# A later second gather and an earlier split of the first gathered rows in a mixture-of-experts block

## What is computed

```python
def hierarchical_moe(h2, w_rg, w_re, w_gate, w_up, w_down):
    ...
    eid = g_sel[:, None] * EXPERTS_PER_GROUP + top_i
    ...
    def expert_block(args):
        xb, e = args
        return (jax.nn.silu(xb @ w_gate[e]) * (xb @ w_up[e])) @ w_down[e]
```

## Time and profile before

| | us |
|---|---|
| median of 3 runs | 1263.93 |
| lowest and highest run | 1262.71, 1267.04 |
| span of the profiled execution | 1263.3 |
| TensorE busy in the span | 1220.1 |
| VectorE busy | 959.5 |
| ScalarE busy | 681.5 |
| GpSimd busy | 257.5 |

### The profile page before, as it was taken

The page is one execution under the profiler, slowest core; times in us unless marked ns, Lnnn a source line. Parts: engine busy times, 40 slices in busy tenths (PEclk is TensorE's granted clock), DMA queues, the critical chain, the costliest instruction groups (busy, mean ns, idle before and its releaser), DMA issues. The chain is left out here.

```text
span 1263.3 us, 18788 instructions
## 1 busy us (share of the span) xinstructions
PE 1220.1 (97%) x7332; PEld 1013.2 (80%) x7332; DVE 959.5 (76%) x1173; ACT 681.5 (54%) x819; POOL 257.5 (20%) x193
## 2 busy tenths in 40 slices
PE   4799999999999999999989999999999999999997
PEld 1799888888788887888778888888888888788883
DVE  1756554432578888666789999999999999999977
ACT  3932212111456666422256777777777777677734
POOL 0000000001100000100020634535355272622110
PEclk9899999999999999999989999999999999999999
DMA  9649844435566775431379999999999999999949
GB/s 380 252 178 311 286 138 142 170 121 169 185 221 185 156 189 133 151 110 51 137 264 358 379 386 392 375 389 380 382 385 377 385 375 395 382 363 378 384 150 359
DMA packets 96620, 344.36 MB, mean 273 GB/s; under 512 B 18522, under 2 KB 46866, under 8 KB 68883
## 3 DMA queue, kind: packets, MB, share of 16 engines
q1 hardware_dynamic: 75603, 311.91, 67.8%
q10 hardware_dynamic: 11696, 14.44, 3.9%
q0 software_dynamic: 9232, 16.80, 3.6%
HBM read 314.24 MB, written 39.34 MB: 280 GB/s over the span
## 5 line engine op out<-in xcount | busy, mean ns | idle before, releaser
L2262 DVE TENSOR_TENSOR w_low<-raw,w_high 128x2048 fp32r<-128x2048 f32 x128 | 291.7, 2299 | 6.0 <-ACT w_high L2194 5.1
L2194 ACT ACTIVATE w_high<-raw 128x2048 fp32r<-128x2048 f32 x128 | 240.8, 1908 | 4.9 <-PEq L1388 3.8
L2076 PE MATMUL p_gu<-w_high,x_high 128*128 128x512 f32 x504 | 202.5, 402 | 0.0
L2078 PE MATMUL p_gu<-w_high,x_low 128*128 128x512 f32 x504 | 197.2, 391 | 0.0
L2077 PE MATMUL p_gu<-w_low,x_high 128*128 128x512 f32 x504 | 196.3, 390 | 0.0
L2262 DVE TENSOR_TENSOR w_low<-arena,w_high 128x2048 fp32r<-128x2048 f32 x62 | 142.6, 2303 | 25.5 <-ACT w_high L2194 25.5
L2134 POOL DMA_INDIRECT y_rows<-arena,row x31 | 66.9, 2158 | 311.1 <-DVE arena L2293 309.6
L2194 ACT ACTIVATE w_high<-arena 128x2048 fp32r<-128x2048 f32 x62 | 118.2, 1906 | 0.0
L2078 PEld LDWEIGHTS p_gu<-w_high,x_low 128*128 128x128 f32 x504 | 94.6, 188 | 20.9
L2077 PEld LDWEIGHTS p_gu<-w_low,x_high 128*128 128x128 f32 x504 | 94.9, 188 | 18.0
L2076 PEld LDWEIGHTS p_gu<-w_high,x_high 128*128 128x128 f32 x504 | 95.2, 189 | 17.7
(11 more groups left out here) (426 smaller groups left out, 2532.1 us busy)
## 6 DMA issues: line engine op xcount, KB each, us to landing
raw<-in_w_gate SPq DMA_DIRECT2D x64, 1024.0 KB, 7.9
raw<-in_w_up SPq DMA_DIRECT2D x64, 1024.0 KB, 8.1
arena<-in_w_down SPq DMA_DIRECT2D x62, 1024.0 KB
raw<-in_w_ada SPq DMA_DIRECT2D x24, 1024.0 KB, 7.6
x<-qk_rows SPq DMA_DIRECT2D x6, 1664.0 KB, 8.3
raw<-in_w_chunks SPq DMA_DIRECT2D x9, 1024.0 KB, 5.7
qk_rows<-x SPq DMA_DIRECT2D x18, 512.0 KB, 2.6
mod<-x ACTq DMA_DIRECT2D x48, 128.0 KB, 3.2
```

The lines of the kernel that those rows point to most:

```text
L2076: pe.matmul(dst, high, w_high, start=start, stop=False)
L2078: return pe.matmul(dst, low, w_high, start=False, stop=stop)
L2194: act.activation(x.high[i % SPLITS][:], x.raw[b][:, :], ACT.Copy).then_inc(high_ok, 1)
L2262: dve.tensor_tensor(x.low[i % SPLITS][:], x.raw[home(n, j)][:, :], x.high[i % SPLITS][:], ALU.subtract).then_inc(low_ok, 1)
```

## The change

Three lines are moved and one wait is new. The gather of expert 1 is no longer issued at the end of `mix_and_route` but at the start of GpSimd's stream in `main_experts`, behind a wait for the landing of the gather of expert 0. On ScalarE the two halves of expert 0's rows are split before chunk 3 instead of after it.

```diff
@@ mix_and_route, gpsimd
                 pool.wait_ge(listed_ok, 1)
-                for n in range(2):
-                    gather(pool, a, s, n)
+                gather(pool, a, s, 0)
                 pool.wait_ge(coded, 4)
@@ main_experts, gpsimd
             steps = Counter(pool, over_ready)
+            pool.wait_ge(gathered[0], 16)
+            gather(pool, a, s, 1)
             pool.wait_ge(x_turned, 1)
             gather(pool, a, s, 2)
@@ main_experts, scalar
             split(0, 2)
+            x_split_halves(0)
             split(0, 3)
-            x_split_halves(0)
             split(1, 0)
```

## The result

| | before | changed |
|---|---|---|
| median, us (20 runs each) | 1263.93 | 1267.49 |
| lowest run | 1261.57 | 1262.94 |
| span of the profiled execution | 1263.3 | 1262.2 |

What follows compares the result with a forecast made beforehand. TensorE, nearly without idle time through the expert loop, was taken to bound the kernel. Gains and costs of 0 plus a 1.2 us stall from the moved gather gave 1263.93 + 1.2 = 1265.1 us, range 1262.6 to 1267.3.

Steps and rivals of the forecast that it cites:

- First gather, gain 0: Seam between routing and experts: expert 0's gather lands no sooner, has 2.7 us to spare behind TensorE's filler; gain 0.
- Block boundary: Boundary at 648.04 does not move, since TensorE's event, not GpSimd's second issue, is last; gain 0, at most 0.3 us.
- ScalarE's exchange, cost 0: Halves ahead of chunk 3 still start at 652.02; chunk 3 comes later but has 4.5 us of cover; cost 0.
- The moved gather: Expert 1's gather: issue 649.4 to 651.2, landing 8.0 us later at 659.2, wanted at 658.03; stall 1.2 us.
- The rival by which the gather would interleave at once: Moved gather shares the queue with weights at once or finds it lighter, lands near 654.1, hidden; 1263.9 us, chance 0.26.
- They move with TensorE: Expert loop: two late gathers of later experts, 1.9 us of idle time, shift with TensorE, so early delay is not recovered.
- The range: Whole-kernel time 1262.6 to 1267.3 us, from the lowest run shown below to the slow late-landing case above.
- rival (b): Moved gather lands as late as 661.2 and pushed-back weights become late for ScalarE; costs 3.2 us, 1267.1 us, chance 0.10.
- Rival V: Follow-up rival at the second expert's turning: landing varies between runs, idle 3 us or more, median +3 us; no chance given.
- The time outside the span: Whole kernel: median of three runs 1263.93 against profiled span 1263.3, so 0.6 us taken to lie outside the span.

Runs made afterwards that it cites:

- The short filler: TensorE's filler behind the boundary cut from 30 to 6 transposes, early gathers, ScalarE's exchange, against before: 1261.54 to 1264.49 us, ratio 0.9982; second timing 0.9976.
- the split alone: Only ScalarE's two halves moved ahead of chunk 3, gathers as before, against before: 1266.63 to 1265.79 us, ratio 1.0000.

## Why the prediction was right in its step and wrong in its range

**First gather, gain 0: right.** TensorE's filler still stood right ahead of the first turning, which starts 3.30 or 3.31 us behind the filler's first transpose in all executions with 30 transposes. The short filler showed how much lay there: 2.0 us at the first products, 1.3 us at the second turning.

**Block boundary: right.** GpSimd's second issue was gone and the boundary did not come sooner. That alone proves little, since in the changed profile VectorE's boundary event is the late one (647.8, TensorE's 647.0): its subtraction started 0.6 us later, and TensorE's filler ran partly at the full clock (a mean of 0.91 from 645 to 646, and 0.50 there in before). A second profile of before settles it:

```profile
644.93 2.31 POOL L1888 DMA_INDIRECT arena<-h_rows,token  x1 [0.30 <-issue]
646.75 3.47 PE L291 MATMUL p_gu<-ident 128*128 128x128 f32 x30 [2.24 <-PEq L1388]
```

TensorE starts the new block 0.5 us before GpSimd's issue ends at 647.24. The block at L1388 is built with `no_gpsimd_drain=True`; without it the boundary may well behave otherwise, which no run shows.

**ScalarE's exchange, cost 0: right** in the profiles; the split alone gave a ratio of 1.0000, with an interval of 2 us to either side.

**The moved gather: right, with two errors that cancel.** The issue was to start at 649.4 and started at 650.02, since the first gather had itself been issued 0.6 us later in this execution (644.75 for 644.14). It was to last 1.8 us and lasted 1.25; both are the same rule, the end of VectorE's subtraction plus 0.9, and the end came at 651.27 for the forecast's 651.2. From there to landing it took 8.1 us for 8.0. The stall of 1.2 us was measured as 1.2 us on the average of five executions. The choice of the 8.0 was partly luck: it was taken from the fourth gather for its like size, but the same 0.39 MB took 6.3 us when issued 2.5 us later, so the size does not decide it. The rival by which the gather would interleave at once fell: two packets in 3 us.

**"They move with TensorE": wrong.** I took the 1.9 us at two late gathers of later experts as fixed to the program. There are none of them in one execution of before and 3.4 us in another. The expert loop's idle time is a draw of each execution.

**The range: wrong.** This is the step that failed. The upper end, 1267.3, was rival (b)'s 1267.1 with next to nothing for scatter, although I had seen three runs that differ by 4.3 us. The term that the sum put at nothing is how far a median of such runs can stand off. Before against before gave medians of 11 or 12 runs 0.35 us under and 0.14 us over its own; but before's median itself went from 1263.93 to 1265.79 between timings. Four later timings of the changed kernel stood -0.5, +1.7, +1.1 and +0.4 us against before (from the medians), +0.7 on average, beside the +3.6 of the first. Drawing again and again from the single runs of the four gives -0.1 to +1.5 us for that average (95%): a stall of 1.2 us fits, 3.6 us do not, and the times alone would not even prove a stall. That rests on the distance between the turnings. The other 2.4 us of the first comparison are not explained by any profile: in no profiled execution of seven with the moved gather at its place was the idle time over 1.2 us. Rival V, longer stalls in some executions, is not shown and not excluded, because only one execution of a timing is profiled, and none above 1268 us of the changed kernel was caught. The granted clock is not the reason (a mean of 0.990 over the 20 runs, 0.990 to 0.991 in the four later timings). Whether the chip of the first comparison is, was not tried. That stays open.

**The time outside the span: misread.** The prediction set the median of three runs against the span of one profiled execution and called the difference of 0.6 us the time outside it. Within one execution it is 1.8 or 1.9 us (1264.07 and 1262.2 for the changed kernel). The sum did not need it.

## What to carry to other kernels

A transfer that is moved to where its queue is quiet for the reader of the program may land behind bulk loads that start in between: here 4.3 us later at its issue (650.02 for 645.68) became 8.2 at its landing, from 651.2 to 659.4. Ask of a filler ahead of a wait first whether it hides the wait; here a transfer was tuned that had over 2 us to spare, and cutting the filler gave more than either placement. Look at the granted clock when a filler is cut. Where executions of one kernel differ by more than the effect, the spacing of two events in the trace measures it to a tenth of a us, while medians of a dozen runs do not.

## What the runs showed of the hardware

- The issue of a gather on GpSimd ends about 0.9 us after the VectorE subtraction (SBUF operands, 128x2048) that is running when it starts, whether it starts early or late in it: 2.31 us in before (end 647.99, subtraction to 647.11), 1.25 us and 2.50 us after the change, with ends that lie 0.14 and 0.13 us ahead of the first turning. In the whole trace of before, 41 indirect transfers (gathers and scatters) are issued while such a weight subtraction runs, and all end 0.85 to 1.02 us behind it.
- In a block built with `no_gpsimd_drain=True` the boundary does not wait for GpSimd's issue in progress: GpSimd's event was at 647.8 with the issue lasting to 647.99, and in another execution TensorE started the next block at 646.75 with the issue lasting to 647.24.
- A gather into a queue full of weight transfers starts about 3 us after the end of its issue, into an empty one 0.7 us. The same 0.39 MB landed 9.4 us after its issue started in the first case and 4.2 us in the second.
- Executions of one kernel differ in where the granted clock falls: in one it is 0.57 on average over 3.5 us near the end, with 0.50 (1.2 GHz) from 1237 to 1239, after TensorE had idled 2.19 us; in another it is 1.00 there, after 1.86 us. Eight matmuls took 5.37 us in the first and 3.67 in the second.
